# Second block's expert weights in a ring of nine places instead of six, experts in a plain chain, h added by identity products

## The chip, the cores and the metric

One Trainium2 chip, one of its cores. The metric is the device time of one execution in microseconds (us), the median of several runs; lower is better.

## The reference, cut to what matters

Two transformer blocks run one after the other on 256 tokens of width 1024, all in f32. The first has differential attention, a pooling mixer, 32 experts (top 4) and a gated embedding. The second has windowed attention, a gated recurrence, and the mixture of experts that the change is about:

```python
def hierarchical_moe(xn, w_rg, b_rg, w_re, b_re, w_gate, w_up, w_down):
    ...
    # a group of 8 experts by argmax, in it the top 2; gate_w by token
    ...
    def expert_block(args):
        xb, e = args
        h = jax.nn.silu(xb @ w_gate[e]) * (xb @ w_up[e])
        return h @ w_down[e]
    ...

# in second_block
        x = x + mixed @ w_out[l]
        hn = rms_norm_2(x, norm2_w[l]).reshape(B * S, D)
        moe = hierarchical_moe(hn, w_router_group[l], b_router_group[l], w_router_expert[l],
                               b_router_expert[l], w_gate_experts[l], w_up_experts[l], w_down_experts[l])
        x = x + moe.reshape(B, S, D).astype(x.dtype)
```

Each of the 32 experts of the second block has three matrices of 1024 by 512 (gate, up) and 512 by 1024 (down), 2 MiB each: 96 loads.

## The kernel before, in words

One program on each engine, written out by hand, with semaphores between them. All weights pass through a ring of `SLOTS = 6` places of 2 MiB in the on-chip memory (`ring`, 16 KiB on each of 128 partitions); SyncE (SP) asks for the loads in program order and waits before each until its place is free. `full[s]` counts landed loads of place s, `free[s]` counts the uses that are over.

Second block. Its dense part runs over sixteen loads (`middle`, L382), `dense2` counts its products. Then `experts(1)` (SP L347 to L358, ScalarE L562, VectorE L1174, TensorE L1556 on) takes over: expert p uses three places, gate, up and down, the even experts places 0 to 2 and the odd ones 3 to 5. SP asks for the first six in the order 0 to 5, each when the dense part has used its place for the last time, then in a loop over pairs of experts in the order gate, up, down.

TensorE per expert p (all 32 experts are run, each on up to 32 tokens):

- `gate_up` (L1653): 64 products over the gate and the up place, into PSUM bank 4.
- `gather_rows` (L1605): the rows of the next expert are picked out of h by a one-hot product; ScalarE copies them (L602), `turn_rows` (L1614) transposes them, VectorE scales them (L1005).
- ScalarE takes the sigmoid of bank 4 (L585), VectorE multiplies twice (L1033, L1035), `hid_turn` (L1670) transposes, ScalarE copies (L594).
- `down` (L1680): 16 products over the down place, into bank 5; ScalarE copies (L598).
- `back_turn` (L1661): the gated one-hot matrix is transposed, ScalarE copies (L589); `scatter` (L1708): 8 products that add the expert's result to banks 0 to 3.

Before, these are overlapped across experts: while expert p's hidden values are being made, TensorE does `down` and `scatter` of expert p-1:

```python
                    def overlapped(p, n, s0, prev=None):
                        gate_up(q, p, *main(n, s0))
                        gather_rows(q, p + 1)
                        if prev:
                            down(q, prev[0], *main(*prev[1:]))
                        turn_rows(q, p + 1)
                        ...
                        hid_turn(q, p)
                        if prev:
                            scatter(q, prev[0])
```

Ahead of the experts `fill` (L1581) writes zeros to banks 0 to 3 by bf16 products of 512 columns, sixteen and then five more, placed where TensorE waits for the router's steps on VectorE and ScalarE. At the end VectorE adds h to the four banks (L1209), 1024 columns twice, and SP stores the two tiles (L388). If more than 32 tokens chose an expert, a loop after the last expert takes the rest; SP, ScalarE and TensorE read its length from memory after their last expert, and no such piece occurs with these inputs.

Of the kernel before, what the change touches and what calls it, by code (L numbers as in the profile page):

```python
# [30 lines left out]
P = 128  # L31
# [6 lines left out]
E = 32  # L38
# [18 lines left out]
def two_blocks(nc, w, out):  # L57
# [11 lines left out]
    with ctx:  # L69
# [69 lines left out]
        wrt2 = scr[:, 5120:5632].rearrange("p (c e) -> p c e", c=DC)  # L139
        part = scr[:, 2048:2304]  # L140
        STRIPS = (4, 2)
        hT = xs[:, :, :].rearrange("p a n -> p (a n)").rearrange("p (c t) -> p c t", t=T)
        squares_out = scr[:, 6400:8448].rearrange("p (a n) -> p a n", a=TT)
        TURN_BANKS = ((2, 3, 6, 7), (0, 1, 2, 3))
# [33 lines left out]

        def slot(s, c, n):
            return ring[:, s, 0:c * n].rearrange("p (c n) -> p c n", c=c)  # L180
# [16 lines left out]
        FULL0 = ([1] * SLOTS, [1 + E + n for n in in_slot])  # L197
        FREE0 = ([0] * SLOTS, [E] * SLOTS)
# [5 lines left out]
        PER = (6, 3)  # L204
        TOPK = (4, 2)
        NR = (32, 36)

        def expert_loads(k, e, s0):
# [14 lines left out]
            for i, name in enumerate((GATES[1], UPS[1])):  # L223
                loads.append((s0 + i, ring[:, s0 + i, :], src(name, "a (p c) n -> p (a c n)")))
            loads.append((s0 + 2, ring[:, s0 + 2, :], src(DOWNS[1], "a (p j) n -> p (a j n)")))
            return loads

        LOADS = ((1,) * 6, (1,) * 3)
        LAST = ({"gate": 1, "up": 3, "down": 5}, {"gate_up": 1, "down": 2})

        PAIR = (1, 2)
# [26 lines left out]
        def stage(eng, k, q, n, s0, name):  # L258

            s = s0 + LAST[k][name]  # L260
            if q[0] == "m":
                eng.wait_ge(free[s], n + 1 + FREE0[k][s])
            else:
                eng.wait_ge(sem(f"over_free{k}_{s}"), n + 1)
# [39 lines left out]
        full = [sem(f"slot_full{s}") for s in range(SLOTS)]  # L304
# [6 lines left out]
        def _(sp):  # L311
# [30 lines left out]
            def experts(k, first):  # L342

                for u in range(PAIR[k]):
                    for s, dst, src in expert_loads(k, E - 1 if k == 0 else u, PER[k] * u):
                        first(s)
                        sp.dma_start(dst, src).then_inc(full[s], 16)  # L347
                if k == 0:
                    for s, dst, src in expert_loads(0, E - 2, 0):
                        sp.wait_ge(free[s], 1)  # L350
                        sp.dma_start(dst, src).then_inc(full[s], 16)
                    sp.wait_ge(sem("list"), 1)
                with sp.Fori(2 if k == 0 else 1, E // PAIR[k]) as n:
                    for u in range(PAIR[k]):
                        e = sp.value_load(lst[0:1, ds(n + ORDER, 1)], min_val=0, max_val=E - 1) if k == 0 else n * PAIR[k] + u
                        for s, dst, src in expert_loads(k, e, PER[k] * u):
                            sp.wait_ge(free[s], n + FREE0[k][s])
                            sp.dma_start(dst, src).then_inc(full[s], 16)  # L358
                sp.wait_ge(sem("list"), k + 1)
                n = sp.value_load(lst[0:1, 0:1], min_val=0, max_val=NLIST)  # L360
                with sp.If(n > 0):
                    with sp.Fori(0, n) as i:
                        e = sp.value_load(lst[0:1, ds(i + 1, 1)], min_val=0, max_val=E - 1)
                        seen = [0] * SLOTS
                        for s, dst, src in expert_loads(k, e, 0):
                            if not seen[s]:
                                sp.wait_ge(free[s], E // PAIR[k] + FREE0[k][s])
                                sp.wait_ge(sem(f"over_free{k}_{s}"), i)
                            seen[s] = 1
                            sp.dma_start(dst, src).then_inc(sem(f"over_full{k}_{s}"), 16)  # L370

                    sp.wait_ge(sem(f"over_free{k}_{PER[k] - 1}"), n)
                    sp.sem_inc(sem("over_left"), 1)

            experts(0, lambda s: sp.wait_ge(sem("proj"), 2 * s + 2) if s < 4 else sp.wait_ge(sem("out1"), 2 * s - 6))
# [8 lines left out]
            experts(1, lambda s: sp.wait_ge(sem("dense2"), last_use[s]))  # L384
# [90 lines left out]
        def _(act):  # L475
# [3 lines left out]
            def norm(k, ready):  # L479

                for a in range(TT):
                    ready(a)
                    act.activation(squares_out[:, a, :] if k else xs[:, a, :], h[:, a, :], ACT.Square,
# [78 lines left out]
            def experts(k, ready):  # L562
                norm((F_NORM, N2_NORM)[k], ready)
                act.wait_ge(sem("partial"), k + 1)
                act.copy(part, bank(4)[:, 0:T]).then_inc(sem("partial_copied"), 1)
# [13 lines left out]
                def sigmoid(q, p, n, s0):  # L579
# [3 lines left out]
                    else:  # L583
                        stage(act, k, q, n, s0, "gate_up")
                        act.activation(act_t[:, 0:128], bank(4)[:, 0:128], ACT.Sigmoid).then_inc(done_by(q, "act", "sigmoid"), 1)  # L585
# [61 lines left out]
                else:  # L647
                    def overlapped(p, n, s0, prev=None):
                        sigmoid(q, p, n, s0)
                        leave_rows(q, p + 1)  # L650
                        if prev:
                            leave_y(q, *prev)
                        leave_hid(q, p)
                        leave_back(q, p)

                    overlapped(0, 0, 0)
                    with act.Fori(0, E // 2 - 1) as n:
                        overlapped(2 * n + 1, n, 3, (2 * n, n, 0))
                        overlapped(2 * n + 2, n + 1, 0, (2 * n + 1, n, 3))
                    overlapped(E - 1, E // 2 - 1, 3, (E - 2, E // 2 - 1, 0))  # L660
# [1517 lines left out]
```

## Time and profile before

| | before |
|---|---|
| median of 3 runs | 1816.21 us (1814.09 to 1817.25) |
| the profiled execution, its own time | 1813.94 us |
| its span in the profile | 1812.1 us |
| TensorE busy | 1701.0 us (94%) |
| VectorE / ScalarE busy | 394.8 us (22%) / 248.5 us (14%) |
| DMA queue of SP | 651.91 MB, 86.6% of 16 engines |
| chain that ended last | TensorE 63%, DMA 34%, VectorE 2% |

The table is one profiled execution beside the median of the runs. Busy times are sums over the whole span; a busy TensorE is not TensorE at its peak, since the ends of its products are modelled. The chain is followed back from the last instruction, at each step to what released it; a share of it for DMA is time in which a load was what the work waited for.

### The profile page before, as it was taken

The page shows a single profiled execution, that of the slowest core. Times are in us where ns is not written, and L with a number is a line of the kernel's source. Part 1 is how long each engine was busy: PE and PEld are TensorE (multiplying, and loading weights), DVE is VectorE, ACT ScalarE, POOL GpSimd, SP SyncE. Part 2 cuts the span into 40 slices and gives each one's busy share as a digit, 9 for nine tenths or more (in the row PEclk, how much of TensorE's full clock was granted, in tenths as well). Part 3 has the DMA queues.
Part 4 walks back from the last instruction along what each step waited for, and adds up shares of the span by engine and source line. Part 5 has one row for each costly group of instructions (what it writes and reads, how often), then busy time and mean ns, then how long its engine had stood idle before and what let it go on. Part 6 is the DMA issues. An engine that isn't in the chain of part 4 may idle for free.

```text
span 1812.1 us, 28778 instructions
## 1 busy us (share of the span) xinstructions
PE 1701.0 (94%) x12185; PEld 772.9 (43%) x12185; DVE 394.8 (22%) x946; ACT 248.5 (14%) x528; POOL 28.0 (2%) x107
## 2 busy tenths in 40 slices
PE   8999999999999999999999999999999888888887
PEld 4543333333333323333333336656456555555554
DVE  3542112121212111112111122432331111111111
ACT  2311111110211101000000012031011111111111
POOL 3020000000000000000000000000000000000000
PEclk9999999999999999999999999999999999999999
DMA  9549999999999997999999995321278999999997
GB/s 315 206 169 430 428 428 428 428 428 428 427 428 428 428 420 321 429 428 429 429 429 428 428 381 186 139 93 47 96 279 373 429 428 428 428 428 428 428 429 300
DMA packets 72727, 655.25 MB, mean 362 GB/s; under 512 B 13184, under 2 KB 14992, under 8 KB 35440
## 3 DMA queue, kind: packets, MB, share of 16 engines
q1 hardware_dynamic: 69936, 651.91, 86.6%
q0 software_dynamic: 528, 1.98, 0.4%
q10 hardware_dynamic: 2224, 0.79, 0.2%
q8 instruction: 30, 0.49, 0.1%
q14 instruction: 9, 0.07, 0.0%
HBM read 653.62 MB, written 1.05 MB: 361 GB/s over the span
## 4 chain that ended last, share of the span: by engine, by line
PE 63%; DMA 34%; DVE 2%; SPq 1%; issue 1%; ACT 0%; DVEq 0%
PE ps L1620 26%; DMA ring<-in_w_up_experts 18%; DMA ring<-in_w_up 15%; PE ps L1925 6%; PE ps L1985 6%; PE ps L1653 4%; PE ps L1447 3%; PE ps L1605 3%; PE ps L1702 2%; PE ps L1680 2%; PE ps L1515 2%; PE ps L1629 1%; PE ps L1614 1%; PE ps L1766 1%; PE ps L1668 1%; SPq L358 1%
## 5 line engine op out<-in xcount | busy, mean ns | idle before, releaser
L1620 PE MATMUL ps<-ring,Z 128*64 128x512 f32 x3072 | 678.6, 595 | 14.4 <-DMA ring<-in_w_up 13.8
L1620 PEld LDWEIGHTS ps<-ring,Z 128*64 128x64 f32 x3072 | 213.4, 137 | 451.2 <-issue 414.6
L1653 PE MATMUL ps<-ring,Z 128*32 128x128 f32 x4096 | 246.7, 408 | 62.7 <-DMA ring<-in_w_gate_experts 33.1
L1653 PEld LDWEIGHTS ps<-ring,Z 128*32 128x32 f32 x4096 | 147.5, 126 | 152.9 <-DMA ring<-in_w_up_experts 44.3
L1985 PE MATMUL ps<-ring,xT 128*128 128x512 f32 (+1 forms) x256 | 105.7, 567 | 0.0
L1605 PE MATMUL ps<-h,Z 128*32 128x256 f32 (+1 forms) x792 | 102.0, 470 | 0.7 <-DVE Z L991 0.7
L1021 DVE TENSOR_SCALAR Z<-ps 128x512 f32<-128x512 f32 x32 | 22.1, 692 | 355.8 <-PE ps L1620 355.8
L1033 DVE TENSOR_TENSOR Z<-Z,ps 128x128 f32<-128x128 f32 x32 | 9.2, 288 | 294.9 <-ACT Z L585 294.9
L1023 DVE TENSOR_SCALAR Z<-ps 128x512 f32<-128x512 f32 x32 | 22.1, 692 | 229.1 <-PE ps L1620 229.1
L1985 PEld LDWEIGHTS ps<-ring,xT 128*128 128x128 f32 x256 | 47.6, 190 | 48.9 <-issue 48.2
L589 ACT COPY Z<-ps 128x256 f32<-128x256 f32 x64 | 23.8, 372 | 323.5 <-PE ps L1661 323.5
L598 ACT COPY Z<-ps 128x256 f32<-128x256 f32 (+1 forms) x63 | 30.0, 477 | 273.1 <-PE ps L1620 229.6
L1702 PE MATMUL ps<-Z 64*128 64x512 f32 x256 | 63.6, 615 | 0.8 <-ACT Z L598 0.8
L1680 PE MATMUL ps<-ring,Z 128*32 128x256 f32 x1024 | 61.5, 379 | 0.0
L1447 PE MATMUL ps<-ring,xT 128*128 128x512 f32 x128 | 57.3, 608 | 3.0 <-DMA ring<-in_w_in 3.0
L1925 PE MATMUL ps<-ring,xT 128*128 128x512 f32 x128 | 56.1, 594 | 1.5 <-DVE xT L1222 0.8
L1005 DVE TENSOR_TENSOR Z<-ps,gcol 128x512 f32<-128x512 f32 (+1 forms) x66 | 36.8, 558 | 88.4 <-PE ps L1614 88.2
L582 ACT ACTIVATE Z<-Z 128x512 f32<-128x512 f32 x32 | 20.2, 630 | 244.5 <-DVE Z L1021 244.5
L1013 DVE TENSOR_SCALAR Z<-iota,Z 128x128 f32<-128x128 f32 x128 | 38.6, 344 | 68.8 <-issue 41.2
L1605 PEld LDWEIGHTS ps<-h,Z 128*32 128x32 f32 (+1 forms) x792 | 36.0, 125 | 36.7 <-issue 24.8
L585 ACT ACTIVATE Z<-ps 128x128 f32<-128x128 f32 x32 | 8.9, 277 | 298.6 <-PE ps L1653 298.6
L1680 PEld LDWEIGHTS ps<-ring,Z 128*32 128x32 f32 x1024 | 36.4, 109 | 19.7 <-issue 0.2
(418 smaller groups left out, 1162.6 us busy)
## 6 DMA issues: line engine op xcount, KB each, us to landing
ring<-in_w_gate SPq DMA_DIRECT2D x64, 2048.0 KB, 18.9
ring<-in_w_up SPq DMA_DIRECT2D x64, 2048.0 KB, 22.0
ring<-in_w_down SPq DMA_DIRECT2D x64, 2048.0 KB, 19.1
ring<-in_w_gate_experts SPq DMA_DIRECT2D x32, 2048.0 KB, 17.0
ring<-in_w_up_experts SPq DMA_DIRECT2D x32, 2048.0 KB, 21.5
ring<-in_w_down_experts SPq DMA_DIRECT2D x32, 2048.0 KB, 13.0
ring<-in_w_in SPq DMA_DIRECT2D x12, 2048.0 KB, 12.6
ring<-in_w_out SPq DMA_DIRECT2D x4, 2048.0 KB, 19.0
```

The source lines that it names most:

```text
L598: act.copy(y[:, 0:(512, 256)[k]], bank((7, 5)[k])[:, 0:(512, 256)[k]]).then_inc(done_by(q, "act", "y"), 1)
L1005: tt(picked[:, 0:DC * CAPS[k]].rearrange("p (c j s) -> p c j s", **by_chunk), bank(6)[:, 0:DC * CAPS[k]].rearrange("p (c j s) -> p c j s", ...
L1013: ts(gated[:, a].rearrange("p (j s) -> p j s", s=CAPS[k]), iota[:, None, 0:CAPS[k]].broadcast_to([P, P // CAPS[k], CAPS[k]]), rank[:, a, d ...
L1447: last = pe.matmul(bank(j % 2), xT[:, c, a * P:(a + 1) * P], slot(u, DC, 512)[:, c, :], start=c == 0, stop=c == DC - 1)
L1515: last = pe.matmul(bank((4, 5, 0, 1)[b]), xT[:, c, a * P:(a + 1) * P], slot(4 + n, DC, 512)[:, c, :], start=c == 4, stop=c == 3)
L1605: last = pe.matmul(bank(6)[n * j:n * (j + 1), 0:P * c].rearrange("p (q c) -> p q c", c=c), one_hot[:, a, 0:n], h[:, a, :].rearrange("p (q ...
L1620: last = pe.matmul(dst[CAP * j:CAP * (j + 1)], lhsT, rhs(j), start=start, stop=True, skip_group_check=True)
L1653: last = pe.matmul(bank(4)[CAP2 * t:CAP2 * (t + 1), P * s:P * (s + 1)], picked[:, chunk * CAP2:(chunk + 1) * CAP2], v[:, c, t:512:4], star ...
L1680: last = pe.matmul(bank(5)[CAP2 * t:CAP2 * (t + 1), 0:T], hid[:, CAP2 * j:CAP2 * (j + 1)], v[:, j, T * t:T * (t + 1)], start=j == 0, stop= ...
L1702: last = pe.matmul(bank(2 * a + j), back[CAP * j:CAP * (j + 1), a * P:(a + 1) * P], y[CAP * j:CAP * (j + 1), :], start=False, stop=True, s ...
L1925: last = pe.matmul(dst, lhs(c), rhs(c), start=c == 0, stop=c == nc_ - 1)
L1985: last = pe.matmul(bank(i % 2)[:, 0:n], tile(a)(c), v[:, c, :], start=c == 0, stop=c == DC - 1)
```

## The change

What it does, in the second block's experts (the first block's expert loop keeps its order and its places):

1. Three more places of 2 MiB: two in the scratch tile `scr`, one in `Z`. `HOME` maps the nine places of three experts to them: 4, 5, 0, 1, 6, 7, 8, 2, 3, the order in which the dense part lets them go. Places 6 to 8 are asked for after `mixed` reaches 4, that is after VectorE's last sum ahead of the output projection. Small tiles that lay in `scr` or in the way (`wrt2`, `part`, the squares of the norm, the activations) move.
2. One semaphore, `used2`, counts all uses over, instead of one for each place.
3. TensorE, ScalarE and VectorE run the experts as a plain chain: `gate_up(p)`, `scatter(p-1)`, `back_turn(p)`, `gather_rows(p+1)`, `hid_turn(p)`, `turn_rows(p+1)`, `down(p)`. TensorE's loop holds three experts, ScalarE's and VectorE's hold one. The last expert is written out by itself, without the rows of a next one.
4. The zero products of `fill` become products of the identity with h, four (then one), so that banks 0 to 3 begin with h. The end is then four copies of 512 columns, two on VectorE and two on ScalarE (after its read of the leftover list's length), and four stores of 256 columns of both tiles.

```diff
+        homes = [ring[:, s, :] for s in range(SLOTS)] + [scr[:, 0:SLOT], scr[:, SLOT:2 * SLOT], Z[:, 0, 0:SLOT]]
...
+        HOME = (range(SLOTS), (4, 5, 0, 1, 6, 7, 8, 2, 3))
+        TRIPLE = 3
...
+            def fill_second():
+
+                for u in range(TRIPLE):
+                    for s, dst, src in expert_loads(1, u, PER[1] * u):
+                        home = HOME[1][s]
+                        if home < SLOTS:
+                            sp.wait_ge(sem("dense2"), last_use[home])
+                        else:
+                            sp.wait_ge(sem("mixed"), 4)
+                        sp.dma_start(dst, src).then_inc(full[home], 16)
+                with sp.Fori(1, E // TRIPLE) as n:
+                    for u in range(TRIPLE):
+                        for s, dst, src in expert_loads(1, n * TRIPLE + u, PER[1] * u):
+                            sp.wait_ge(sem("used2"), n * 9 + (s - 8))
+                            sp.dma_start(dst, src).then_inc(full[HOME[1][s]], 16)
+                for u in range(E % TRIPLE):
...
-            for a in range(TT):
-                sp.wait_ge(sem("moe_out"), 4 + a + 1)
-                sp.dma_start(out[0, a * P:(a + 1) * P, :], h[:, a, :]).then_inc(sem("stored"), 16)
-            sp.wait_ge(sem("stored"), 16 * TT)
+            rows_out = out[0].rearrange("(a p) n -> p a n", p=P)
+            for b, who, n in ((2, "d2_copied", 17), (0, "moe_out", 5), (3, "d2_copied", 18), (1, "moe_out", 6)):
+                sp.wait_ge(sem(who), n)
+                sp.dma_start(rows_out[:, :, T * b:T * (b + 1)], h[:, :, T * b:T * (b + 1)]).then_inc(sem("stored"), 16)
...
-                    def overlapped(p, n, s0, prev=None):
+                    def chained(p, n, s0, ahead=True):
                         sigmoid(q, p, n, s0)
-                        leave_rows(q, p + 1)
-                        if prev:
-                            leave_y(q, *prev)
+                        leave_back(q, p)
+                        if ahead:
+                            leave_rows(q, p + 1)
                         leave_hid(q, p)
-                        leave_back(q, p)
...
+                if k == 1:
+                    for b in range(2, 4):
+                        act.copy(h[:, :, T * b:T * (b + 1)], bank(b).rearrange("p (a n) -> p a n", a=TT)).then_inc(sem("d2_copied"), 1)
...
-                    for a in range(TT):
-                        row = h[:, a, :].rearrange("p (t n) -> p t n", t=4)
-                        tt(row, ps[:, 0:4, 256 * a:256 * (a + 1)], row, ALU.add).then_inc(sem("moe_out"), 1)
+                    for b in range(2):
+                        dve.tensor_copy(h[:, :, T * b:T * (b + 1)], bank(b).rearrange("p (a n) -> p a n", a=TT))\
+                            .then_inc(sem("moe_out"), 1)
...
+                            pe.matmul(by_tile, ident[:, :], h[:, :, T * (b % 4):T * (b % 4 + 1)], start=True, stop=True)
+
+                fill((10, 4)[k])
...
+                    def chained(p, n, s0, prev, ahead=True):
                         gate_up(q, p, *main(n, s0))
-                        gather_rows(q, p + 1)
...
+                        if prev is not None:
+                            scatter(q, prev)
+                        back_turn(q, p)
+                        if ahead:
+                            gather_rows(q, p + 1)
+                        after(pe, k, q, "act", "back", p)
                         hid_turn(q, p)
...
+                        if ahead:
+                            turn_rows(q, p + 1)
+                        down(q, p, *main(n, s0))
+
+                    chained(0, 0, 0, None)
+                    with pe.Fori(0, E // TRIPLE) as n:
+                        chained(3 * n + 1, n, 3, 3 * n)
+                        chained(3 * n + 2, n, 6, 3 * n + 1)
+                        chained(3 * n + 3, n + 1, 0, 3 * n + 2)
+                    chained(E - 1, E // TRIPLE, 3, E - 2, False)
                     scatter(q, E - 1)
```

TensorE in the second block's experts, before: expert 0 and the first of the pair in the loop. L1653 is `gate_up`, L1605 `gather_rows`, L1680 `down`, L1614 `turn_rows`, L1670 `hid_turn`, L1708 `scatter`, L1661 `back_turn`; the loop starts at L1900.

```order
L1653 MATMUL ps<-ring,Z 32x128 x64
L1605 MATMUL ps<-h,Z 32x256 x8
L1614 MATMUL ps<-ident,Z 128x128 x2
L1670 MATMUL ps<-ident,Z 128x128
L1661 MATMUL ps<-ident,Z 128x128 x2
...
L1605 MATMUL ps<-h,Z 32x256 x8
L256 REGISTER_ALU
L1680 MATMUL ps<-ring,Z 32x256 x16
L1614 MATMUL ps<-ident,Z 128x128 x2
```

The same engine at the same place, now; expert 0 and the beginning of expert 1. The lines have moved: L1687 is `gate_up`, L1695 `back_turn`, L1639 `gather_rows`, L1704 `hid_turn`, L1648 `turn_rows`, L1714 `down`, L1742 `scatter`.

```order
L1687 MATMUL ps<-ring,Z 32x128 x64
L1695 MATMUL ps<-ident,Z 128x128 x2
L1639 MATMUL ps<-h,Z 32x256 x8
L1704 MATMUL ps<-ident,Z 128x128
L1648 MATMUL ps<-ident,Z 128x128 x2
L1714 MATMUL ps<-ring,Z 32x256 x16
...
L1687 MATMUL ps<-ring,Z 32x128 x32
L1687 MATMUL ps<-scr,Z 32x128 x32
L259 REGISTER_ALU
L1742 MATMUL ps<-Z 128x256 x8
```

`down` of expert 0 now stands ahead of `gate_up` of expert 1, where before it stood behind it.

SyncE's requests for the first loads of the experts, now:

```order
L374 DMA ring<-in_w_gate_experts 128x4096 [waits dense2]
L374 DMA ring<-in_w_up_experts 128x4096 [waits dense2]
L374 DMA ring<-in_w_down_experts 128x4096 [waits dense2]
L374 DMA ring<-in_w_gate_experts 128x4096 [waits dense2]
L374 DMA scr<-in_w_up_experts 128x4096 [waits mixed]
L374 DMA scr<-in_w_down_experts 128x4096 [waits mixed]
L374 DMA Z<-in_w_gate_experts 128x4096 [waits mixed]
L374 DMA ring<-in_w_up_experts 128x4096 [waits dense2]
L374 DMA ring<-in_w_down_experts 128x4096 [waits dense2]
```

Before there were six of them, all waiting on `dense2`; the three that wait on `mixed` are new.

## Rows read from the trace of the kernel before

**Rows 1.** The page: the DMA engines' busy share in 40 slices, in tenths.
```profile
DMA  9549999999999997999999995321278999999997
```

**Rows 2.** Windows: us, busy by engine (instructions), granted PE clock, DMA share, GB/s.
```profile
1359.00:1364.00 5.00, 4.96 (x87) 3.26 (x76) 0.78 (x3) 1.11 (x4) 0.00 (x0) 1.00 0.00 0
...
1380.00:1790.00 410.00, 347.25 (x5508) 213.20 (x5503) 57.65 (x196) 46.45 (x140) 0.00 (x0) 1.00 1.01 428
```

**Rows 3.** Timeline of TensorE: up half of experts 3 and 31 (start, us, idle before).
```profile
1382.17 3.88 PE L1653 MATMUL ps<-ring,Z 128*32 128x128 f32 x64 [0.73 <-DMA ring<-in_w_up_experts]
...
1793.29 3.88 PE L1653 MATMUL ps<-ring,Z 128*32 128x128 f32 x64 [0.90 <-DMA ring<-in_w_up_experts]
```

**Rows 4.** Timeline of SyncE's queue: the first requests after expert 0 has begun.
```profile
1346.91 0.35 SPq L358 DMA_DIRECT2D ring<-in_w_gate_experts  x1
1350.42 0.34 SPq L358 DMA_DIRECT2D ring<-in_w_up_experts  x1
1363.38 0.33 SPq L358 DMA_DIRECT2D ring<-in_w_down_experts  x1
```

**Rows 5.** Timeline of TensorE: expert 0's products, then expert 2 whole.
```profile
1342.77 7.62 PE L1653 MATMUL ps<-ring,Z 128*32 128x128 f32 x128
...
1364.98 0.44 PE L1661 MATMUL ps<-ident,Z 128*128 128x128 f32 x2
1365.35 7.57 PE L1653 MATMUL ps<-ring,Z 128*32 128x128 f32 x128
1372.68 1.17 PE L1605 MATMUL ps<-h,Z 128*32 128x256 f32 x16
1373.62 1.96 PE L1680 MATMUL ps<-ring,Z 128*32 128x256 f32 x32
1375.51 0.50 PE L1614 MATMUL ps<-ident,Z 128*128 128x128 f32 x2
...
1376.15 1.15 PE L1708 MATMUL ps<-Z 32*128 32x256 f32 x16
1377.23 0.44 PE L1661 MATMUL ps<-ident,Z 128*128 128x128 f32 x2
1377.60 3.84 PE L1653 MATMUL ps<-ring,Z 128*32 128x128 f32 x64
```

**Rows 6.** Timeline of ScalarE and VectorE: what hands expert 0 on.
```profile
1350.43 0.28 ACT L585 ACTIVATE Z<-ps 128x128 f32<-128x128 f32 x1 [7.71 <-PE ps L1653]
...
1351.06 0.29 DVE L1035 TENSOR_TENSOR Z<-Z,ps 128x128 f32<-128x128 f32 x1
1351.35 0.37 ACT L602 COPY Z<-ps 128x256 f32<-128x256 f32 x1 [0.64 <-PE ps L1605]
...
1352.42 0.27 ACT L594 COPY Z<-ps 128x128 f32<-128x128 f32 x1 [0.70 <-PE ps L1670]
```

**Rows 7.** Timeline of the end, all engines.
```profile
1801.87 1.93 PE L1680 MATMUL ps<-ring,Z 128*32 128x256 f32 x32
...
1804.39 1.15 PE L1708 MATMUL ps<-Z 32*128 32x256 f32 x16 [0.58 <-ACT Z L598]
1805.81 2.36 DVE L1209 TENSOR_TENSOR h<-ps,h 128x1024 f32<-128x1024 f32 x2 [5.09 <-PE ps L1708]
1807.06 1.47 SPq L388 DMA_DIRECT2D out<-h  x2
```

**Rows 8.** First block, VectorE: two reads of a list, a jump, then L1013.
```profile
608.27 0.60 DVE L1013 TENSOR_SCALAR Z<-iota,Z 128x128 f32<-128x128 f32 x2 [1.21 <-issue]
```

**Rows 9.** TensorE ahead of the experts: output projection's last tile, zeros, ranks.
```profile
1321.33 7.03 PE L1925 MATMUL ps<-ring,xT 128*128 128x512 f32 x16
...
1332.62 3.62 PE L1581 MATMUL ps<-zeros 128*128 128x512 bf16 x16
1337.09 0.41 PE L1588 MATMUL ps<-Z,tri 128*128 128x32 f32 x2 [0.85 <-DVE Z L968]
```

**Rows 10.** DMA issues: the router's load from GpSimd, KB, us to landing.
```profile
scr<-in_w_router_expert POOLq DMA_DIRECT2D x1, 128.0 KB, 6.1
```

More of the change, by code:

```diff
@@ L138, in two_blocks @@
         wrt = moe[:, 0:256].rearrange("p (c e) -> p c e", c=DC)
-        wrt2 = scr[:, 5120:5632].rearrange("p (c e) -> p c e", c=DC)
-        part = scr[:, 2048:2304]
+        wrt2 = Z[:, 0, 4096:4608].rearrange("p (c e) -> p c e", c=DC)
+        act_g2, act_t2, act_h2 = (Z[:, 0, 4096 + P * k:4096 + P * (k + 1)] for k in range(3))
+        parts = (scr[:, 2048:2304], Z[:, 0, 4608:4864])
         STRIPS = (4, 2)
@@ L143, in two_blocks @@
         squares_out = scr[:, 6400:8448].rearrange("p (a n) -> p a n", a=TT)
+        n2_squares = (Z[:, 1, 3840:4864], scr[:, 8192:9216])
         TURN_BANKS = ((2, 3, 6, 7), (0, 1, 2, 3))
@@ L302, in two_blocks @@
             at += n
-        full = [sem(f"slot_full{s}") for s in range(SLOTS)]
+        full = [sem(f"slot_full{s}") for s in range(SLOTS + 3)]
         free = [sem(f"slot_free{s}") for s in range(SLOTS)]
@@ L340, in _, with fill_first @@
             assert n_late[0] == N_LATE
[L342 to L346, printed above, removed]
-                        sp.dma_start(dst, src).then_inc(full[s], 16)
[L348 to L358, printed above, removed]
+            def fill_first():
+                for s, dst, src in expert_loads(0, E - 1, 0):
+                    if s < 4:
+                        sp.wait_ge(sem("proj"), 2 * s + 2)
+                    else:
+                        sp.wait_ge(sem("out1"), 2 * s - 6)
+                    sp.dma_start(dst, src).then_inc(full[s], 16)
+                for s, dst, src in expert_loads(0, E - 2, 0):
+                    sp.wait_ge(free[s], 1)
+                    sp.dma_start(dst, src).then_inc(full[s], 16)
+                sp.wait_ge(sem("list"), 1)
+                with sp.Fori(2, E) as n:
+                    e = sp.value_load(lst[0:1, ds(n + ORDER, 1)], min_val=0, max_val=E - 1)
+                    for s, dst, src in expert_loads(0, e, 0):
+                        sp.wait_ge(free[s], n)
+                        sp.dma_start(dst, src).then_inc(full[s], 16)
@@ L564, in experts @@
                 act.wait_ge(sem("partial"), k + 1)
-                act.copy(part, bank(4)[:, 0:T]).then_inc(sem("partial_copied"), 1)
+                act.copy(parts[k], bank(4)[:, 0:T]).then_inc(sem("partial_copied"), 1)
                 if k == 1:
@@ L1176, in experts, with chained @@
                 else:
-                    def overlapped(p, n, s0):
-                        choose(q, p + 1)
-                        if n is not None:
-                            after(dve, k, q, "pe", "back", p - 1)
+                    def chained(p, n, s0, ahead=True):
                         gate(q, p, p, p)
-                        if n is not None:
-                            after(dve, k, q, "pe", "hid", p - 1)
+                        if ahead:
+                            choose(q, p + 1)
                         activate(q, p, n, s0)
-                        gather(q, p + 1)
-                    overlapped(0, None, 0)
-                    with dve.Fori(0, E // 2 - 1) as n:
-                        overlapped(2 * n + 1, n, 3)
-                        overlapped(2 * n + 2, n + 1, 0)
-                    overlapped(E - 1, E // 2 - 1, 3)
+                        if ahead:
+                            gather(q, p + 1)
+                    with dve.Fori(0, E - 1) as p:
+                        chained(p, p, 0)
+                    chained(E - 1, E - 1, 0, False)
                 n = dve.value_load(lst[0:1, 0:1], min_val=0, max_val=NLIST)
@@ L1571, in experts @@
                 for a in range(TT):
-                    last = pe.matmul(bank(6)[:, NR[k] * a:NR[k] * (a + 1)], part[:, a * P:(a + 1) * P],
+                    last = pe.matmul(bank(6)[:, NR[k] * a:NR[k] * (a + 1)], parts[k][:, a * P:(a + 1) * P],
                                      (sel[:, 0:E], sel2[:, :])[k], start=True, stop=True)
@@ L1720, in filled @@
                     def filled(s):
-                        pe.wait_ge(full[s0 + s], 16 * LOADS[k][s] * (n + 1) + 16 * FULL0[k][s0 + s])
-                    return s0, filled, lambda s: free[s0 + s]
+                        home = HOME[k][s0 + s]
+                        pe.wait_ge(full[home], 16 * (n + 1) + 16 * FULL0[k][home])
+                    return s0, filled, lambda s: free[s] if k == 0 else sem("used2")
                 q = f"m{k}_"
-                fill((2, 3)[k])
+                fill((2, 1)[k])
                 gather_rows(q, 0)
@@ L1732, in experts @@
                     .then_inc(sem("listing_pe"), 1)
-                fill((2, 1)[k])
+                fill((2, 0)[k])
                 turn_rows(q, 0)
-                fill((2, 1)[k])
+                fill((2, 0)[k])
                 pe.wait_ge(sem("listing_dve"), 2 * k + 2)
```

104 lines of the change are left out of this document (50 added, 54 removed).

## The prediction

> **What bounds the kernel now.** First the page: nearly all of the span is a stretch in which the DMA engines are full, with one hollow in slices 25 to 30, the second block's dense part [rows 1]. Then the windows: from 1380 us to 1790 us the share is 1.01 at 428 GB/s, while TensorE is busy 347 of 410 us [rows 2]. So the second block's experts end when the last weights have landed. TensorE's timeline gives the pace: the up half of expert 3 resumes at 1382.17, that of expert 31 at 1793.29, each released by its load [rows 3]; 411.12 us for 28 experts are 14.68 us an expert, 4.894 a load.
>
> What counts then is when this stream starts, how many loads it has left, and whether it pauses. The SyncE queue shows that. Expert 0 begins at 1342.77 without waiting for weights [rows 5], with six loads in the ring; the seventh is asked for at 1346.91, when the gate place is free, the eighth at 1350.42, the ninth only at 1363.38, 12.96 us later [rows 4]. It waits for the down place, which expert 0 frees behind expert 1's `gate_up`. Between 1359 and 1364 the DMA share is 0.00 [rows 2]. Seventh and eighth load keep the engines full for 9.8 us, so the ninth could have followed the seventh by 9.8 us; it followed by 1363.38 - 1346.91 = 16.5 us: a **pause of 6.7 us**. Afterwards the stream never stops.
>
> From the ninth request to the resumption of expert 3's up half are 18.8 us for three loads: 14.7 and 4.1 of start and landing [rows 3, 4].
>
> **The change part by part.**
>
> *Three more places.* 87 loads instead of 90 are left when expert 0 frees its first place: 3 x 4.894 = **14.7 us** less, if all nine are there or moving at 1343. Gate and up of expert 0 go to the two places that the dense part leaves first; the three new ones are asked for when `mixed` is 4, ahead of the output projection; the last of the nine waits for that projection's last tile, which runs from 1321.33 for 7.03 us [rows 9]. One load asked at 1328.4 lands some 9 us later, about 1337. So all are there.
>
> *The down place comes free in turn.* In the plain chain `down(0)` stands right behind expert 0's handoffs: `gate_up` ends near 1350.4, the pieces below bring the end of `down` to about 1355.3. The stream needs the ninth request by 1346.91 + 9.8 = 1356.7, plus what start-up leaves over. The pause closes, **6.7 us**. Margin 1.4 us at least; expert 1's gate place follows at about 1359, the stream needs it at 1361.6.
>
> Check: before, load 89 of 90 (up of expert 31) is 89 x 4.894 = 435.6 after 1346.91, with 4.1 and the pause 1793.3; measured 1793.29. Now it is number 86: 1346.91 + 420.9 + 4.1 = **1771.9**, 21.4 us earlier.
>
> *The plain chain on TensorE.* Expert 2, which waits for no load, takes 1365.35 to 1377.60 = 12.25 us: `gate_up` 7.33, `gather_rows` 0.94, `down` 1.89, the two turns 0.64, `scatter` 1.08, `back_turn` 0.37 [rows 5]. The chain keeps these and gives up the cover of `down`. Behind `gate_up` come sigmoid and two multiplications, from 1350.43 to 1351.06 + 0.29 = 1351.35, 0.92 us [rows 6]; `scatter`, `back_turn` and `gather_rows` take 2.39: covered. The row copy of ScalarE (0.37) starts 0.04 after the gather's modelled end of 1.17 [rows 5, 6], so `turn_rows` can start about 1.63 after the gather's start; gather and `hid_turn` fill 0.94 + 0.30. A wait of 0.4. The hidden copy (0.27) ends with `turn_rows`. VectorE's scaling of the next rows is under `down`. Estimate **12.65 us** an expert; bounds 12.25 (nothing shown) and about 15 (every handoff of rows 6, the copies of `back` and y too, uncovered). I take 12.65, since the row copy is the only handoff with less work in front of it than it takes. Against a load pace of 14.68 that is hidden: TensorE starts at 1342.8 with nine places full and is caught by the stream near expert 16. It would set the end only above 13.67 (worked out below).
>
> *Three uses of a place in `scr` and `Z`.* Same 16 KiB rows on 128 partitions, same products: nothing. The waits on one counter cost SyncE register instructions, hidden while a load moves.
>
> *The router's weights* are asked for by GpSimd at the same moment as four loads. Before they landed in 6.1 us [rows 10]. They are used behind the output projection, whose four tiles of 7.03 us [rows 9] lie between the request and the use: 28 us. Even behind all of four loads, 19.6 us, they would be there after 25.7.
>
> *Identity products.* Eight products of 512 f32 columns take 7.03 us [rows 9], 0.88 each; four take 3.5, the sixteen zero products took 3.62, and TensorE then waited 0.85 more for VectorE [rows 9]. The fifth stands where three zero products and later two stood. **0**, bounds -0.3 and +0.3. If more, all that follows is late by it, the seventh request too.
>
> *The end.* Before, from the resumption at 1793.29 VectorE starts its sums 12.52 later, the second store is asked at about 1808.2, 14.9 later, and the span ends 18.8 later [rows 3, 7]. Now, behind the same load: up half 3.7; `scatter(30)` 1.08; `back_turn` with its copy, no longer covered by a gather, 0.44 + 0.37 and 0.1 between = 0.9; `hid_turn` with its copy 0.27 + 0.27 + 0.1 = 0.6; `down` to `scatter` 2.52, `scatter` to VectorE 1.42 [rows 7]. Sum 10.2. ScalarE then reads the list's length before it copies. VectorE's gap around two such reads and a jump is 1.21 [rows 8]; bounds for one read with its branches 0.3 and 1.5, taken 1.0, the whole gap less a little. Two copies at about 0.6 (half of 2.36 / 2): the first store is asked at 11.9, the last of four at 13.1, and 3.9 as before to the end: 17.0. That is **1.8 us** less; bounds 0 and 4 (smaller stores land sooner).
>
> Sum: 14.7 + 6.7 + 1.8 = 23.2 us. The profiled execution took 1813.94: 1790.7. The median of before is 2.3 above that execution; from it 1816.2 - 23.2 = **1793.0 us**, which I forecast. A change of under 0.2% (3.6 us) could not be told from none.
>
> **The rivals.**
>
> *The pause stays or moves.* If `down(0)` ends 2 us later than worked out, or if the stream pauses once for expert 1, up to 6.7 us are lost: 1793.0 + 6.7 = 1799.7. For it: the margin is an estimate. Against it: SyncE asks in the order in which places come free, so nothing is queued behind a late one. 0.10.
>
> *TensorE becomes the bound.* With X us an expert the end is 1342.8 + 32 X, then 0.6 to the last `scatter` and 8.2 to the end: 1351.6 + 32 X. That passes the forecast's 1788.9 at X = 13.67. At X = 14, 1799.6 of span, 1803.7 by the median. It needs 1.35 us an expert more than I find in rows 5 and 6. 0.05.
>
> *Slower: the loops' jumps and the exposed handoffs stall TensorE.* Equal to before at X = 14.39, slower by 0.2% from X = 14.5; at X = 15, the upper bound, the span would be 1831.6, the median 1835.7. Its place is the wait ahead of `hid_turn` and `turn_rows` and the jump at the loop's end, 31 jumps on ScalarE and VectorE, nine on TensorE. Against it: expert 2 to 3, over a jump of the pair loop, goes from `back_turn` to `gate_up` in 0.37, as expert 1 to 2 does without one [rows 5]. 0.03. The Trainium skill (Runtime: NRT & Kernel Launch, Instruction fetch mechanics) says that a jump to a target outside the two pages held forces a fetch by DMA before execution goes on. By it each jump could stall an engine while the DMA engines are full. The trace does not agree at TensorE's loop of two experts; a loop of three is not shown.
>
> *It does not do what it says.* If the three new places are asked for later than thought, the stream simply moves at 1343 instead of resting, and only the wait of an expert could cost. If an extra place held nothing, 14.7 would be missing: 1807.7. 0.02.
>
> **How the numbers follow.** Forecast as worked out, with the bounds of its terms: 0.80, from 1788 (tail 4, and the faster execution of before as the measure) to 1796. The range reaches up over the pause rival, which with the forecast makes 0.90: 1787.5 to 1800.5. The other three cases, 0.10, are left out; of them the jumps and handoffs (0.03) are slower, 0.02 of TensorE as the bound comes to rest within 0.2%, and the rest is faster. Faster by over 0.2%: 0.95; within: 0.02; slower: 0.03.
>
> **What would show it.** Right: the seventh request near 1346.9, the ninth by 1357, no window after 1347 with a DMA share under 0.95; expert 31's up half resumes near 1772; the span ends 17 us after. Experts 1 to 10 at about 12.7 us each, with a wait of 0.4 ahead of `turn_rows` and none for DMA. Wrong: a TensorE that in the last ten experts waits for no load (then it is the bound), an idle DMA between 1355 and 1370, or router products that start after 1330.

## The result, and the profile after

The change takes 1792.01 us (median of 4 runs, 1790.87 to 1793.43) against 1816.0 us before; the ratio is 0.9873 with a 95% interval of 0.9861 to 0.9885. That is 24.0 us by the medians, where 23.2 were forecast (1793.0 us). The profiled execution took 1790.87 us, its span is 1789.0 us.

The windows of the change, at the places of [rows 2] and around them (us, busy by engine, granted clock, DMA share, GB/s):

```profile
1328.00:1343.00 15.00, 12.63 (x96) 6.68 (x98) 11.09 (x57) 5.86 (x13) 0.00 (x0) 1.00 0.39 141
1343.00:1347.00 4.00, 4.00 (x76) 2.71 (x72) 1.06 (x5) 0.00 (x0) 0.00 (x0) 1.00 0.17 33
1347.00:1355.00 8.00, 7.76 (x125) 4.52 (x121) 2.02 (x7) 2.42 (x6) 0.00 (x0) 1.00 0.97 385
...
1359.00:1364.00 5.00, 4.79 (x71) 2.47 (x63) 0.57 (x2) 1.05 (x4) 0.00 (x0) 1.00 0.98 419
```

Where the DMA share was 0.00 between 1359 and 1364 it is 0.98; between 1347 and 1765 no window falls under 0.97. The shares of 0.39 and 0.17 ahead of it are new (0.93 before between 1328 and 1343) and harmless: all nine places are full, and the stream rests until expert 0 frees one.

SyncE's requests in the change, to be read beside [rows 4]:

```profile
1328.21 0.33 SPq L374 DMA_DIRECT2D ring<-in_w_down_experts  x1
1345.93 0.34 SPq L379 DMA_DIRECT2D ring<-in_w_gate_experts  x1
1349.47 0.34 SPq L379 DMA_DIRECT2D ring<-in_w_up_experts  x1
1353.75 0.33 SPq L379 DMA_DIRECT2D ring<-in_w_down_experts  x1
1357.58 0.33 SPq L379 DMA_DIRECT2D ring<-in_w_gate_experts  x1
```

The third request behind expert 0 comes 7.8 us after the first, where it came 16.5 us after it [rows 4]. The stream needs it within 9.8.

TensorE at expert 2, the piece that answers to [rows 5], and the pair of products that ends the stream, to be read beside [rows 3]:

```profile
1366.21 3.94 PE L1687 MATMUL ps<-Z 128*32 128x128 f32 x64
1369.92 3.94 PE L1687 MATMUL ps<-ring,Z 128*32 128x128 f32 x64
1373.78 1.15 PE L1742 MATMUL ps<-Z 32*128 32x256 f32 x16
1374.86 0.44 PE L1695 MATMUL ps<-ident,Z 128*128 128x128 f32 x2
1375.23 1.12 PE L1639 MATMUL ps<-h,Z 128*32 128x256 f32 x16
1376.28 0.33 PE L1704 MATMUL ps<-ident,Z 128*128 128x128 f32 x1
1376.84 0.50 PE L1648 MATMUL ps<-ident,Z 128*128 128x128 f32 x2 [0.23 <-ACT Z L634]
1377.28 1.93 PE L1714 MATMUL ps<-ring,Z 128*32 128x256 f32 x32
1379.03 7.52 PE L1687 MATMUL ps<-ring,Z 128*32 128x128 f32 x128
...
1771.06 3.88 PE L1687 MATMUL ps<-scr,Z 128*32 128x128 f32 x64 [0.95 <-DMA scr<-in_w_up_experts]
```

Expert 2 takes 12.82 us (1366.21 to 1379.03), 0.57 more than expert 2 before; experts 1 and 3 take 12.70. The one new wait is ahead of `turn_rows`, for the row copy, as worked out, but 0.23 us long and not 0.4. Expert 31's up half resumes at 1771.06; 1771.9 was forecast, 1793.29 was before. TensorE's waits over the experts show from where the stream leads (waited for, us in total, times, longest):

```profile
PE ps L1687 <- DMA ring<-in_w_up_experts: 9.9, 11, 1.0
PE ps L1648 <- ACT Z L634: 7.3, 31, 0.2
PE ps L1687 <- DMA ring<-in_w_gate_experts: 6.2, 11, 0.7
PE ps L1687 <- DMA scr<-in_w_up_experts: 6.0, 6, 1.0
PE ps L1687 <- DMA Z<-in_w_gate_experts: 3.2, 5, 0.7
```

Seventeen waits for an up half and sixteen for a gate half, 25.3 us, where before there were 29 and 28, 62.7 us: experts 0 to 14 wait for no load, and from the up half of expert 15 on, at 1536.14, the stream leads.

The end of the change, beside [rows 7]:

```profile
1780.05 1.15 PE L1742 MATMUL ps<-Z 32*128 32x256 f32 x16 [0.58 <-ACT Z L630]
1781.47 1.29 DVE L1239 COPY h<-ps 128x512 f32<-128x512 f32 x2 [5.52 <-PE ps L1742]
1781.98 1.07 ACT L706 COPY h<-ps 128x512 f32<-128x512 f32 x2 [2.07 <-PE ps L1742]
1782.59 2.00 SPq L419 DMA_DIRECT2D out<-h  x4
```

From the resumption VectorE starts 10.4 us later (12.5 before), but from there the span ends 7.5 us later (6.3 before).

### The profile page after: what moved, and what is told of

It is laid out like the page before. It is cut to its first block, busy times and chain, and to the rows that moved or that the text cites. A ratio compares the mean times of both kernels' runs of the same rounds, so it can differ in the third digit from the quotient of the medians.

```text
span 1789.0 us, 28857 instructions
## 1 busy us (share of the span) xinstructions
PE 1707.8 (95%) x12156; PEld 768.8 (43%) x12156; DVE 391.3 (22%) x943; ACT 284.7 (16%) x559; POOL 28.0 (2%) x107
## 4 chain that ended last, share of the span: by engine, by line
PE 68%; DMA 29%; DVE 2%; ACT 1%; issue 0%; SPq 0%; ACTq 0%; DVEq 0%
PE ps L1654 27%; DMA ring<-in_w_up 16%; DMA scr<-in_w_up_experts 13%; PE ps L1687 7%; PE ps L1959 6%; PE ps L2019 6%; PE ps L1478 3%; PE ps L1639 3%; PE ps L1736 2%; PE ps L1546 2%; PE ps L1714 1%; PE ps L1648 1%; PE ps L1663 1%; PE ps L1801 1%; PE ps L1742 1%; PE ps L1702 1%
## 5 line engine op out<-in xcount | busy, mean ns | idle before, releaser
L1687 PE MATMUL ps<-ring,Z 128*32 128x128 f32 x2752 | 166.0, 409 | 16.1 <-DMA ring<-in_w_up_experts 9.9
L1687 PEld LDWEIGHTS ps<-ring,Z 128*32 128x32 f32 x2752 | 105.0, 127 | 73.2 <-DMA ring<-in_w_up_experts 15.4
L1639 PE MATMUL ps<-h,Z 128*32 128x256 f32 (+1 forms) x776 | 99.8, 468 | 0.4 <-DVE Z L1026 0.3
L1687 PE MATMUL ps<-scr,Z 128*32 128x128 f32 x704 | 42.7, 409 | 6.0 <-DMA scr<-in_w_up_experts 6.0
L1639 PEld LDWEIGHTS ps<-h,Z 128*32 128x32 f32 (+1 forms) x776 | 29.3, 117 | 37.9 <-issue 29.7
L1687 PE MATMUL ps<-Z 128*32 128x128 f32 x640 | 38.9, 410 | 3.2 <-DMA Z<-in_w_gate_experts 3.2
## 6 DMA issues: line engine op xcount, KB each, us to landing
ring<-in_w_gate_experts SPq DMA_DIRECT2D x22, 2048.0 KB, 34.2
```

What stands on the lines that cost most here:

```text
L1639: last = pe.matmul(bank(6)[n * j:n * (j + 1), 0:P * c].rearrange("p (q c) -> p q c", c=c), one_hot[:, a, 0:n], h[:, a, :].rearrange("p (q ...
L1687: last = pe.matmul(bank(4)[CAP2 * t:CAP2 * (t + 1), P * s:P * (s + 1)], picked[:, chunk * CAP2:(chunk + 1) * CAP2], v[:, c, t:512:4], star ...
```

## The experiments

The theory: the end is set by the first request behind expert 0, the number of loads left then (4.894 us each) and the pauses of the stream; TensorE is hidden below some 13.7 us an expert. The part ahead of the second block's experts moves by up to 3.5 us from profile to profile: the request for place 0 comes at 1280.21 in the change and between 1279.3 and 1282.8 in the others. Spans are therefore also given **counted from that request**: 531.7 before (it stands at 1280.39), 508.8 for the change. The stream's own part is the time from the first request behind expert 0 to the resumption of expert 31's up half: 446.4 before, 425.1 in the change.

**Six places with the plain chain.**

```diff
-        HOME = (range(SLOTS), (4, 5, 0, 1, 6, 7, 8, 2, 3))
-        TRIPLE = 3
+        HOME = (range(SLOTS), (4, 5, 0, 1, 2, 3))
+        TRIPLE = 2
```

> The change with six places (4, 5, 0, 1, 2, 3) and a loop of two experts; chain, identity products and end stay. Theory (stream: the end is set by the first request behind expert 0, the loads left, and pauses): 90 loads left instead of 87, no pause, so the span is that of the change plus 3 x 4.894 = 14.7: 1803.7 us, and the window from 1355 to 1364 us shows a full DMA. Rival (the three places alone bring the gain, the chain only costs): the pause of 6.7 us is still there and the span is about 1810.

Measured: 1803.2 us, ratio 0.9933 (0.9916 to 0.9949); span 1801.3, counted 521.6. The requests of this run:

```profile
1345.45 0.35 SPq L379 DMA_DIRECT2D ring<-in_w_gate_experts  x1
1349.06 0.34 SPq L379 DMA_DIRECT2D ring<-in_w_up_experts  x1
1353.35 0.33 SPq L379 DMA_DIRECT2D ring<-in_w_down_experts  x1
```

No pause, with six places: the third request comes 7.9 us after the first, and the DMA share between 1359 and 1364 is 1.03. The stream's own part is 6.9 us shorter than before (439.5 against 446.4), with the same 90 loads left. The three places are worth 521.6 - 508.8 = 12.8 us. In the stream's own part it is 14.4: 1784.94 - 1345.45 = 439.5 against 425.1. The landing of the last stores takes 1.5 of it back, 6.0 us behind VectorE's start here and 7.5 in the change. The rival's 1810 falls.

**Nine places with the overlapped experts of before.**

```diff
-                        after(pe, k, q, "act", "back", p)
-                        hid_turn(q, p)
+                        if prev:
+                            down(q, prev[0], *main(*prev[1:]))
                         if ahead:
                             turn_rows(q, p + 1)
-                        down(q, p, *main(n, s0))
...
+                        if prev:
+                            scatter(q, prev[0])
```

ScalarE and VectorE follow the same order, and each place has a semaphore of its own again.

> The change with nine places, but TensorE, ScalarE and VectorE run the experts overlapped as before. Theory: the twelfth load waits for the down place that expert 0 frees behind the gate and up products of expert 1, near 1362.5, so a pause of 6 to 7 us comes back whatever the number of places; with about 2 us more behind the last load, since the down products of expert 30 stand there, the span is 1797 to 1798 us. Rival (nine places give the stream enough in hand, the pause does not come back, and TensorE is faster by 0.5 us an expert): 1789 us or less.

Measured: 1801.4 us, ratio 0.9914 (0.9898 to 0.9931); span 1799.6, counted 517.1, that is 8.3 us behind the change, as expected (8 to 9). The stream's own part is 6.8 us longer (431.9), from the resumption to VectorE it takes 1.1 us more (11.5), and the rest is the landing of the last stores. The pause is back: SyncE's second and third request in this run,

```profile
1351.75 0.34 SPq L381 DMA_DIRECT2D ring<-in_w_up_experts  x1
1364.71 0.33 SPq L381 DMA_DIRECT2D ring<-in_w_down_experts  x1
```

and the window of the same stretch, with a DMA share of 0.16:

```profile
1359.00:1364.00 5.00, 5.00 (x92) 3.56 (x88) 0.57 (x2) 0.65 (x2) 0.00 (x0) 1.00 0.16 66
```

**The same, asked for in the order in which that schedule frees the places.** Gate and up of expert p stand ahead of down of expert p-1 in SyncE's queue, nothing else changes:

```diff
+                    ask(n * 3, n, 0, (0, 1))
+                    ask(n * 3 + (-1), n + (-1), 2, (2,))
+                    for u in (1, 2):
+                        ask(n * 3 + u, n, u, (0, 1))
+                        ask(n * 3 + (u - 1), n, u - 1, (2,))
```

> Nine places and the overlapped experts of e2, but SyncE asks in the order in which that schedule frees the places: gate and up of expert p ahead of down of expert p-1. Counted from the request for place 0, e2's span ended 517.1 us later and the change's 508.8. Theory (the pause comes from a request that waits behind a place not yet free, not from the overlapped schedule itself): the pause of 6.7 us goes, the third request behind expert 0 comes near 9 us after the first instead of 16.5, and the end is 510 to 511 us after the request for place 0. Rival (the plain chain is what brings it): 517.

Measured: 1792.3 us, ratio 0.9873 (0.9855 to 0.989), the same as the change; span 1791.0, counted 509.2.

SyncE's requests in this run, its third one now for a gate place:

```profile
1347.38 0.33 SPq L380 DMA_DIRECT2D ring<-in_w_gate_experts  x1
1351.16 0.33 SPq L380 DMA_DIRECT2D ring<-in_w_up_experts  x1
1357.83 0.33 SPq L380 DMA_DIRECT2D ring<-in_w_gate_experts  x1
```

The third request comes 10.5 us after the first, where near 9 was expected and 9.8 needed. The pause is gone but for a remainder: the DMA share between 1359 and 1364 is 0.94. Here the up half of expert 31 is load 85 and not 86, so by the pace of the loads it should resume 4.9 us sooner behind the first request than in the change; it does so by 3.2 (422.0 against 425.1). The end comes out the same because TensorE now waits for the last down load (0.84 us) and has only that expert's `down` and `scatter` behind it. So what closes the pause is that no request waits behind one whose place comes free later than its own. With nine places the plain chain is one way to that, and costs nothing that could be told; it is not needed. Six places asked in this way, with the overlapped experts, were not run.

**Nine places in the order of their numbers.**

```diff
-        HOME = (range(SLOTS), (4, 5, 0, 1, 6, 7, 8, 2, 3))
+        HOME = (range(SLOTS), (0, 1, 2, 3, 4, 5, 6, 7, 8))
```

> The change with HOME in the order 0 to 8, nothing else. Theory: places 3 to 8 are asked for behind place 3, at 1328.2; the stream then never rests, and has 6 + 87 = 93 loads to move from there: 1328.2 + 4.1 + 93 x 4.894 = 1787.4 for the last landing, against 1776.0 now, so the span is 1789.0 + 11.4 = 1800.4 us. Rival (what counts is that nine places are there, and the resting time between 1337 and 1346 us takes the later requests): 1789 us, since the loads would all be in time for the experts that use them.

Measured: 1803.2 us, ratio 0.9931 (0.9915 to 0.9948); span 1799.9, counted 520.6: 11.8 us behind the change, 11.4 expected. Six requests leave together behind place 3:

```profile
1312.65 0.33 SPq L374 DMA_DIRECT2D ring<-in_w_down_experts  x1
1327.26 0.33 SPq L374 DMA_DIRECT2D ring<-in_w_gate_experts  x1
1327.64 0.44 SPq L374 DMA_DIRECT2D ring<-in_w_up_experts  x1
...
1329.78 0.46 SPq L374 DMA_DIRECT2D Z<-in_w_down_experts  x1
```

Six loads take 29 us to move (6 x 4.894), so the engines are still busy with them when expert 0 frees its first place: the DMA share is 0.97 between 1344 and 1346, where it is 0.00 in the change. The order in which nine places are asked for is worth 11.8 us, about as much as the three places (12.8).

**TensorE's slack: three and seven zero products more in every expert.** They are added to bank 0 behind `scatter`:

```diff
+                        for _ in range(3):
+                            pe.matmul(bank(0).rearrange("p (a n) -> p a n", a=TT), nothing[:, 0:P],
+                                      nothing[:, None, :].broadcast_to([P, TT, T]), start=False, stop=True, skip_group_check=True)
```

> The change with three zero products of 512 bf16 columns (0.226 us each by the row of sixteen in 3.62) in every expert, added to bank 0, behind the scatter: TensorE's share of an expert goes from 12.8 to 13.4 us. Theory (the stream sets the end, TensorE has slack up to about 13.7): the stream still catches TensorE before the last expert and the span stays at 1789.0, within the 1.5 us by which the landing of the last stores has differed. Rival (TensorE is on the path, each 0.1 us an expert costs 3): 1789 + 32 x 0.65 = 1810 us.

> The same with seven zero products in every expert: TensorE's share becomes 12.8 + 1.5 = 14.3 us. Theory: now above the threshold, no expert waits for a load, and the end is set by TensorE: start of expert 0 at 1341.9 + 32 x 14.3 + 0.6 + 1.4 + 7.5 = 1809 us. Rival (no such threshold, the products hide in the waits for the sigmoid and the copies): 1789 us.

Measured: with three, 1791.3 us (ratio 0.987, 0.9855 to 0.9885) and a span of 1789.0, counted 509.5 against 508.8: no difference that could be told, while an expert takes 13.43 us (1393.54 to 1406.97) and TensorE's busy time between 1380 and 1765 us rises from 354.8 to 370.1. With seven, 1809.0 us (ratio 0.9964, 0.9951 to 0.9977), span 1807.6, counted 525.4. TensorE's waits with seven:

```profile
PE ps L1648 <- ACT Z L634: 7.2, 31, 0.2
PE ps L1742 <- ACT Z L630: 0.6, 1, 0.6
```

No wait for a load is left; 1771.64 to 1785.94 is one expert, 14.30 us, and TensorE sets the end. The threshold lies between 13.4 and 14.3 us; 13.67 was worked out.

**The zero products, the two sums and the two stores of before, on top of the change.**

```diff
-                fill((10, 4)[k])
+                fill((10, 16)[k])
...
-                    for b in range(2):
-                        dve.tensor_copy(h[:, :, T * b:T * (b + 1)], bank(b).rearrange("p (a n) -> p a n", a=TT))\
-                            .then_inc(sem("moe_out"), 1)
+                    for a in range(TT):
+                        row = h[:, a, :].rearrange("p (t n) -> p t n", t=4)
+                        tt(row, ps[:, 0:4, 256 * a:256 * (a + 1)], row, ALU.add).then_inc(sem("moe_out"), 1)
```

> The change with the zero products of before (16, 3, 1, 1), VectorE's two sums of h and the two stores of whole rows; places and chain stay. Theory: expert 0 begins 0.9 us later, since with zero products the granted clock between 1328 and 1343 us falls to 0.89 and the first gather takes 1.75 us instead of 1.12; behind VectorE's start the old end takes 6.3 us where the new one takes 7.5. Span 1789.0 + 0.9 - 1.2 = 1788.7 us. Rival (the new end is the shorter one, as I had forecast, by about 2 us): 1791 to 1792 us. Rival for the start (it is a matter of fewer products and not of the clock): the clock stays at 1.00 and the first gather at 1.12 us.

Measured: 1792.6 us, ratio 0.9869 (0.9852 to 0.9885); span 1791.5, counted 508.7 against 508.8. VectorE starts at 1784.00, the span ends 7.5 us later. The clock stays at 1.00 and the first gather takes 1.12 us, with zero products: my theory for the start falls, and the number of products does nothing either. The 1788.7 expected is missed; the rival's 1791 to 1792 is met by the span only because the request for place 0 comes 2.6 us later here (1282.77) than in the change. Sums or copies, two stores or four: nothing that could be told. What the new end gains comes from the chain: from the resumption to VectorE it takes 10.4 us with both ends, 12.5 before.

**The kernel before once more.**

> The kernel before once more, for its profile. In the recorded profile the granted clock falls to 0.50 near 1340 to 1342 us, ahead of expert 0, and the first request behind expert 0 comes 66.5 us after the request for place 0, where the change and every variant of it have 65.7 to 65.8 and a clock of 1.00. Theory (the fall belongs to the kernel before): it is there again and costs 0.8 us. Rival (it comes and goes from execution to execution): the clock stays at 1.00 and the distance is 65.7.

Measured: one execution of 1815.73 us, span 1813.9, counted 532.1, clock 1.00 (2.4 GHz) from 1338 to 1344 us. In the first profile of before the granted clock is 0.50 (1.2 GHz) between 1340 and 1342:

```profile
1340.00:1342.00 2.00, 2.00 (x18) 0.83 (x10) 0.99 (x8) 0.93 (x2) 0.00 (x0) 0.50 1.04 442
```

Ahead of that TensorE runs three zero products, waits 0.34 us for VectorE and begins the first gather, which takes 1.75 us; in this run the same products stand there, and the gather takes 1.12. The request for place 0 is at 1281.80, the first behind expert 0 at 1347.55: 65.75 between them, as in the change (65.72). So the fall of the clock and its 0.8 us came with one execution of the kernel and not with the other. VectorE starts its sums at 1806.37 here, and the span ends 7.5 us later, where the recorded profile has 6.3: the landing of the last stores differs by that much for the same kernel.

**Two stores of 512 columns.**

```diff
-            for b, who, n in ((2, "d2_copied", 17), (0, "moe_out", 5), (3, "d2_copied", 18), (1, "moe_out", 6)):
+            for b, who, n in ((0, "moe_out", 6), (1, "d2_copied", 18)):
```

> The change with two stores of 512 columns instead of four of 256. Theory (the four requests follow each other by 0.5 us, and the last one, 2.6 us behind VectorE's first copy, sets the end): the last request comes 0.6 to 1 us earlier, the landing behind it differs from run to run by more (3.3 to 5.1 us in the profiles so far), so no difference in the median can be told: 1791 to 1792 us. Rival (rows of 1 KB are what makes the last landing late): 1790 us or less, and a landing below 4 us.

Measured: 1791.9 us, ratio 0.9873 (0.9856 to 0.9889), counted 508.9: no difference. VectorE starts at 1783.17 and the span ends 7.8 us later. Rows of twice the length show no sooner landing; in one profile, beside a spread of 6.0 to 7.9 us over all, a difference under 1 us would not show.

**A tenth place, used once.** `xs` and `xT` become one tile, which takes the gate weights of expert 3; experts 0 to 3 are written out, the other places turn on by one load.

```diff
-        homes = [ring[:, s, :] for s in range(SLOTS)] + [scr[:, 0:SLOT], scr[:, SLOT:2 * SLOT], Z[:, 0, 0:SLOT]]
+        homes = [ring[:, s, :] for s in range(SLOTS)] + [scr[:, 0:SLOT], scr[:, SLOT:2 * SLOT], Z[:, 0, 0:SLOT], xsT[:, :]]
...
+                g3, u3, d3 = expert_loads(1, 3, 0)
+                sp.wait_ge(sem("partial"), 2)
+                sp.dma_start(homes[9], g3[2]).then_inc(full[9], 16)
+                for i, (_, _, src) in enumerate((u3, d3)):
+                    sp.wait_ge(sem("used2"), i + 1)
```

> The change with a tenth place in the tiles xs and xT, used once, for the gate weights of expert 3, asked for when the router's products have read xs, near 1331. Theory: that load moves while the stream rests, 86 loads are left behind expert 0's first place instead of 87, and the last one lands 4.9 us earlier: span 1784.1 us. TensorE stays hidden: at 12.8 us an expert its end is 1341.9 + 409.6 + 9.5 = 1761. Rival (a load that starts at 1331 comes in the way of the last weights of expert 2 or lands after 1346, and the first request waits for it): 1787 to 1789 us.

> Ten places and two stores together, the candidate for the best version. Theory: as e8, 1788 to 1789 us, the stores adding 0 to 1 us of gain. Rival as for e7: 1787 or less.

Measured: 1788.8 us, ratio 0.9851 (0.9838 to 0.9865), span 1787.1, counted 505.5; with two stores 1787.1 us, ratio 0.9852 (0.9835 to 0.9869), span 1784.8, counted 504.2.

```profile
1329.59 0.33 SPq L377 DMA_DIRECT2D ring<-in_w_down_experts  x1
1332.92 0.33 SPq L380 DMA_DIRECT2D xsT<-in_w_gate_experts  x1
1347.22 0.33 SPq L383 DMA_DIRECT2D ring<-in_w_up_experts  x1
```

These are SyncE's requests in the run with four stores. The tenth load moves while the stream would rest: between 1342 and 1344 us the DMA share is 0.04, and the first request behind expert 0 comes 65.6 us after that for place 0, as in the change (65.7). So the first request does not wait for it, and the rival's reason falls, though the medians lie in its range. The gain is 3.3 and 4.6 us by the counted spans, 3 to 5 by the medians, where 4.9 were expected. The intervals of the two ratios overlap that of the change, so that it is faster than the change rests on the counted spans and on the stream's own part, 421.6 and 421.7 against 425.1: 3.5 us in both runs. The 1.3 us between the two runs are the landing of the last stores (7.9 and 6.5 us behind VectorE's start), not the number of stores. Why the stream gains 3.5 and not 4.9 was not found; the engines move as much as in the change, 427 GB/s over the 420 us behind the first request in both profiles, so it is not their pace.

## Why the prediction was right

- **Three places, 14.7 us.** Six places with the chain are 14.4 us later from first request to resumption. Right.
- **The down place in turn, 6.7 us.** From first request to resumption six places with the chain take 6.9 us less than before, and nine places without it 6.8 more than the change; the DMA share in the window is 0.98 with it and 0.16 without. Right in size. The reason as I put it, "the down place comes free in turn" by the plain chain, was narrower than what the runs show: asking in the order in which the overlapped schedule frees the places gives the same time.
- **The start of expert 0.** The step on the identity products said 0, with 0.3 either side. In the change expert 0 starts 61.66 us after the request for place 0, in the second profile of before 61.66 too, in the first 62.38, with the fall of the clock. Right: nothing.
- **The chain, 12.65 us an expert, hidden.** Measured 12.70 and 12.82 in turn. The wait ahead of `turn_rows` is 0.23 and not 0.4, since the gather and `hid_turn` ahead of it take 1.38 and not 1.24; in expert 2 `gate_up` takes 7.57 and not 7.33. TensorE is caught by the stream at expert 15 (16 worked out); the threshold lies between 13.4 and 14.3.
- **The end, 1.8 us.** From resumption to VectorE 10.4 (10.2 worked out). ScalarE's copies start 0.5 us behind VectorE's, where 1.0 was taken; the last request comes at 13.0 (13.1 worked out); but the landing took 4.9 us instead of 3.9, so 0.9 us of gain against the recorded profile. The 3.9 was one draw: the same kernel before shows 7.5 us behind VectorE in its second profile. Against that one the gain of the end is 2.1 us. The term was right, the number for the stores stood on one execution.
- **The router's weights** landed in 9.2 us instead of 6.1 and were in time.
- **The rule on jumps.** In the change the loop of three experts jumps ahead of expert 4: `down(3)` starts at 1389.97 and `gate_up(4)` at 1391.73, 1.76 us later; without a jump, expert 1 to 2, it is 1364.45 to 1366.21, also 1.76. By the Trainium skill (Runtime: NRT & Kernel Launch, Instruction fetch mechanics) a jump out of the pages held stalls the engine. The trace does not show the stall; whether the target of this jump lies outside the pages held, no row tells.

Profile beside profile the span, counted from place 0, is 22.9 us shorter against the first profile of before and 23.3 against the second. The stream's part of it is 21.2 in both, where 21.4 were forecast: that is shown and no luck. Against the first profile two chance differences cancel: 0.8 us at the start, where nothing was forecast and the clock fell in that one execution, and 0.9 us missing at the end, by the landing of the stores. That the sum then met 23.2 within 0.3 us is luck to that extent.

## What to carry to other kernels

In a stretch that a stream of equal loads fills, count three things: when the first request behind the first use goes out, how many loads are left then, and how long the queue is empty. A request that waits for a place which frees later than the next one's cost more here than a whole place (6.8 us against 4.9), and with nine places it was mended in the order of the requests alone. Price a slower schedule on the computing engine against the pace of the loads: up to the threshold it is free, here from 12.7 to at least 13.4 us an expert.

## What the runs showed that I had not expected

- ScalarE's loop over single experts loads its activation table in every turn:

```profile
L617 ACT ACT_TABLE_LOAD x30 | 38.5, 1283 | 0.5
```

  Thirty loads of 1.28 us; the loop over pairs had none, nor had the overlapped loop over triples of the second experiment, and ScalarE's busy time rises from 248.5 to 284.7 us. Why the turns of this loop load it, no run shows. It lies under `gate_up` (7.5 us) and costs nothing here; a shorter expert was not run.
- The median time from request to landing of a gate load went from 17.0 to 34.2 us, at the same 428 GB/s: 34.2 us are seven loads of 4.894, so some seven requests are under way at once (an estimate), where 17.0 us are three and a half.
- From VectorE's start on the last sums or copies to the end of the span it took 6.0 to 7.9 us over all thirteen profiles, with no order by the number of stores or the length of their rows: 6.3 and 7.5 for the kernel before, 6.0 and 7.5 for the six places and the change, which end alike.
